# Strassen loop of a hybrid decoder layer: the operand sums T1 and T3 are made by accumulating transfers instead of VectorE subtractions

## What is computed

```python
D_FF = -(-(8 * D_MODEL) // (3 * 256)) * 256          # 5632
h2 = rms_norm(x, norm2_gain[layer]) * (1 + sc2) + sh2
ffn = (jax.nn.silu(h2 @ ffn_w_gate[layer]) * (h2 @ ffn_w_up[layer])) @ ffn_w_down[layer]
x = x + g2 * ffn
```

## Time and profile before

| | |
|---|---|
| median of 3 executions | 2366.89 us |
| profiled execution | 2369.26 us |
| its span, first to last instruction | 2367.6 us |
| mean granted TensorE clock | 0.993 |
| TensorE matmul busy | 2317.0 us (98%) |
| VectorE busy | 1640.9 us (69%) |
| ScalarE busy | 832.5 us (35%) |
| GpSimd busy | 82.5 us (3%) |
| DMA engines, mean busy share | 49.8% for the queue of SyncE |

### The profile page before, as it was taken

How to read it: one execution, slowest core, us unless ns; L and a number is a source line. 1 busy time by engine, 2 the same in 40 slices (tenths; PEclk the granted TensorE clock), 3 DMA queues, 4 the chain that set the end, 5 groups by cost and what they waited for, 6 DMA issues and landing times.

```text
span 2367.6 us, 28777 instructions
## 1 busy us (share of the span) xinstructions
PE 2317.0 (98%) x10544; PEld 1868.4 (79%) x10544; DVE 1640.9 (69%) x2057; ACT 832.5 (35%) x1147; POOL 82.5 (3%) x80
## 2 busy tenths in 40 slices
PE   6999999999999999999999999999999999999998
PEld 5877787788876788788878787878787878887877
DVE  5976876587757433666777777776868686868683
ACT  4233324343236322343333333333424242424232
POOL 0012100021001000000000000000000000000000
PEclk8999999999999999999999999999999999999999
DMA  9976681677640143234444445353445353545452
GB/s 341 321 263 222 238 306 61 230 237 262 205 145 19 53 161 98 86 110 143 162 134 156 159 151 166 126 179 129 161 133 186 124 180 122 166 142 170 138 164 81
DMA packets 233745, 392.36 MB, mean 166 GB/s; under 512 B 16441, under 2 KB 108063, under 8 KB 232520
## 3 DMA queue, kind: packets, MB, share of 16 engines
q1 hardware_dynamic: 233672, 391.39, 49.8%
HBM read 382.93 MB, written 11.03 MB: 166 GB/s over the span
## 4 chain that ended last, share of the span: by engine, by line
PE 85%; DVE 7%; issue 3%; ACT 2%; DMA 2%; SPq 1%; DVEq 0%; ACTq 0%
PE PS L1057 11%; PE PS L1059 10%; PE PS L1058 10%; PE PS L1112 7%; PE PS L1114 7%; PE PS L1113 7%; PE PS L676 6%; PE PS L678 6%; PE PS L677 6%; PE PS L840 2%; PE PS L683 2%; PE PS L684 2%; PE PS L685 2%; PE PS L816 2%; DVE acc_first L1611 1%
## 5 line engine op out<-in xcount | busy, mean ns | idle before, releaser
L1452 ACT ACTIVATE whi<-stage 128x1024 fp32r<-128x1024 f32 x368 | 390.7, 1062 | 840.6 <-PE PS L1059 444.8
L2000 DVE TENSOR_TENSOR wlo<-stage,whi 128x1024 fp32r<-128x1024 f32 x368 | 449.8, 1224 | 181.0 <-ACT whi L1452 181.0
L1057 PE MATMUL PS<-whi,xc_hi 128*128 128x512 f32 x1216 | 480.8, 395 | 3.2 <-DVE g_tok L2102 2.2
L1059 PE MATMUL PS<-whi,xc_lo 128*128 128x512 f32 x1216 | 474.7, 390 | 0.0
L1058 PE MATMUL PS<-wlo,xc_hi 128*128 128x512 f32 x1216 | 474.3, 390 | 0.0
L1560 DVE TENSOR_TENSOR wlo<-stage,whi 128x1024 fp32r<-128x1024 f32 x136 | 173.1, 1274 | 217.8 <-ACT whi L1230 217.7
L676 PE MATMUL PS<-hhi,whi 128*128 128x512 f32 x768 | 311.3, 405 | 7.5 <-DVE wlo L1560 4.6
L678 PE MATMUL PS<-hhi,wlo 128*128 128x512 f32 x768 | 303.0, 395 | 0.0
L677 PE MATMUL PS<-hlo,whi 128*128 128x512 f32 x768 | 302.8, 394 | 0.0
L1230 ACT ACTIVATE whi<-stage 128x1024 fp32r<-128x1024 f32 x136 | 144.2, 1062 | 437.9 <-PE PS L678 308.6
L1057 PEld LDWEIGHTS PS<-whi,xc_hi 128*128 128x128 f32 x1216 | 228.1, 188 | 77.4 <-DVE wlo L2000 7.5
(11 more groups left out here) (297 smaller groups left out, 2481.7 us busy)
## 6 DMA issues: line engine op xcount, KB each, us to landing
stage<-in_ffn_w_up SPq DMA_DIRECT2D x168, 512.0 KB, 4.0
ada_ring<-in_ada_w SPq DMA_DIRECT2D x128, 512.0 KB, 4.9
stage<-in_ffn_w_gate SPq DMA_DIRECT2D x128, 512.0 KB, 3.7
stage<-in_ffn_w_down SPq DMA_DIRECT2D x88, 512.0 KB, 4.6
stage<-in_w_in SPq DMA_DIRECT2D x80, 512.0 KB, 6.1
ada_first<-in_ada_w SPq DMA_DIRECT2D x64, 512.0 KB, 6.7
stage<-in_w_out SPq DMA_DIRECT2D x32, 512.0 KB, 3.7
xnat<-in_x SPq DMA_DIRECT2D x4, 1024.0 KB, 8.0
```

Source lines behind the costliest of these rows:

```text
L1057: mm(PS[:, b, :], x_hi, w, start=start, stop=False)
L1059: return mm(PS[:, b, :], x_lo, w, start=False, stop=stop)
L1452: f(whi[:, p % NW, :, :].rearrange("p k n -> p (k n)"), slot_of(p), ACT.Copy).then_inc(w_hi, 1)
L2000: v.tensor_tensor(wlo[:, p % NW, :, :].rearrange("p k n -> p (k n)"), slot_of(p), whi[:, p % NW, :, :].rearrange("p k n -> p (k n)").bitca ...
```

## The change

The signs of the scheme are turned so that T1 and T3 are plain sums: T1 = b12 + b11 and T3 = b12 + b22, of the weights as they lie in memory. Then T2 = b22 + T1, and the third and fourth become b11 + T3 and b21 more. The left-hand S1, S2 and S4 change sign to match, and so do U, the first block's product with SiLU (now a `SCALAR_TENSOR_TENSOR` with -1) and the output gate `mod[:, 5, :]`, which is negated once.

T1 and T3 are not made by VectorE any more. SyncE loads the first piece into the slot as before. GpSimd waits for its landing and issues a second transfer of 512 KB from the weights in HBM with `accum_op=ALU.add` into the same slot: `add_weights`, eight for each block, 80 in all, written out one after another without a loop. It also waits for the landing of the accumulating transfer two before it, since two counters (`added`) take turns. ScalarE's copy of a T1 or T3 position, and VectorE's sums that read it, wait for that counter. `sel_ready` and `silu_done` are folded into other counters to make room. The load into position 15 waits for the `wlo` of position 9 and no more for a sum.

```diff
-FREED_BY = {1: 4, 3: 7, 6: 8, 9: 14, 14: 19, 24: 27, 28: 31, 32: 35}
+FREED_BY = {1: 4, 3: 7, 6: 8, 14: 19, 24: 27, 28: 31, 32: 35}
+ADDED = (1, 3, 6, 14, 21, 25, 29, 33)
...
+        def added_at(n, p):
+            return 16 * (ADDED.index(p) // 2 + 1 + 4 * n)
...
                 if p in SUMMED and not down:
                     act.wait_ge(w_sum, sums_of(n, p))
+                elif p in ADDED and not down:
+                    act.wait_ge(added[ADDED.index(p) % 2], added_at(n, p))
                 else:
...
-            then(v.tensor_tensor(t16[:, 0:GCH], mod[:, 3, 0:GCH], mod[:, 3, GCH:KT], ALU.add))
+            then(v.tensor_tensor(t16[:, 0:GCH], mod[:, 3, GCH:KT], mod[:, 3, 0:GCH], ALU.subtract))
+            then(v.tensor_scalar(mod[:, 5, :], mod[:, 5, :], -1.0, None, ALU.mult))
             dve.wait_ge(rh_done, 1)
...
-            def t1(n, j):
-                b11, p, _ = SET1[j]
-                in_stage(n, b11, p)
-                v.tensor_tensor(slot_of(p), slot_of(p), slot_of(b11), ALU.subtract).then_inc(w_sum, 1)
...
-            def t3(n, j):
-                _, p, b22, _ = SET2[j]
-                in_stage(n, p, b22)
-                v.tensor_tensor(slot_of(p), slot_of(b22), slot_of(p), ALU.subtract).then_inc(w_sum, 1)
...
             def b11_plus_t3(n, j):
                 _, t3_at, _, p = SET2[j]
-                in_stage(n, p)
-                dve.wait_ge(w_sum, sums_of(n, t3_at))
+                in_stage(n, t3_at, p)
                 v.tensor_tensor(slot_of(p), slot_of(p), slot_of(t3_at), ALU.add).then_inc(w_sum, 1)
...
-                    v.tensor_tensor(g_tok[:, t, :], PS[:, 4 + t, :], silu_0[:, t, :], ALU.mult
-                                    ).then_inc(bank_free[4 + t], 1)
+                    v.scalar_tensor_tensor(out=g_tok[:, t, :], in0=PS[:, 4 + t, :], scalar=-1.0, in1=silu_0[:, t, :],
+                                           op0=ALU.mult, op1=ALU.mult).then_inc(bank_free[4 + t], 1)
...
+            def add_weights(n, p, w, half, j):
+                i = ADDED.index(p)
+                if n or i >= 2:
+                    pool.wait_ge(added[i % 2], added_at(n, p) - 16)
+                pool.wait_ge(stage_in[p % NRING], landed_at(n, p))
+                g.dma_start(slot_of(p).rearrange("p (k n) -> p k n", k=CK),
+                            w[:, half, CK * j:CK * j + CK, CW * n + CW:CW * n + 2 * CW],
+                            accum_op=ALU.add).then_inc(added[i % 2], 16)
+
+            for n in range(NFB - 1):
+                for j in range(4):
+                    add_weights(n, SET1[j][1], gate_w, 0, j)
+                for j in range(4):
+                    add_weights(n, SET2[j][1], up_w, 1, j)
```

More of the change, by code:

```diff
@@ L283, in hybrid_layer @@
         lags_ready, table_pe, table_sb = sem("lags_ready"), sem("table_pe"), sem("table_sb")
-        silu_done = sem("silu_done")
+        added = [sem(f"added{b}") for b in range(2)]
         mod2_pe, mod2_done = sem("mod2_pe"), sem("mod2_done")
@@ L389, in sums_of @@
         def sums_of(n, p):
-            first = sorted(p for js in SET1 for p in js[1:])
+            first = [js[2] for js in SET1]
             if p in first:
[L393 to L398, removed]
+                return first.index(p) + 1 + 12 * n
+            return 4 + 2 * [js[3] for js in SET2].index(p) + 2 + 12 * n
+        SUMMED = [js[2] for js in SET1] + [js[3] for js in SET2]
         def f_of(f):
@@ L1957, in x_sums @@
                 dve.wait_ge(h2_t, 2 * kp + 2)
-                v.scalar_tensor_tensor(out=b[:, S1, :], in0=b[:, A21, :], scalar=t16[:, kp:kp + 1], in1=b[:, A22, :],
-                                       op0=ALU.add, op1=ALU.add).then_inc(x_sum, 1)
+                v.scalar_tensor_tensor(out=b[:, S1, :], in0=b[:, A22, :], scalar=t16[:, kp:kp + 1], in1=b[:, A21, :],
+                                       op0=ALU.add, op1=ALU.subtract).then_inc(x_sum, 1)
                 v.tensor_tensor(b[:, S3, :], b[:, A11, :], b[:, A21, :], ALU.subtract).then_inc(x_sum, 1)
@@ L1962, in x_sums @@
                 v.scalar_tensor_tensor(out=b[:, S2, :], in0=b[:, S1, :], scalar=low, in1=b[:, A11, :],
+                                       op0=ALU.add, op1=ALU.add).then_inc(x_sum, 1)
+                dve.wait_ge(x_sum, n + 3)
+                v.scalar_tensor_tensor(out=b[:, S4, :], in0=b[:, S2, :], scalar=high, in1=b[:, A12, :],
                                        op0=ALU.subtract, op1=ALU.subtract).then_inc(x_sum, 1)
-                dve.wait_ge(x_sum, n + 3)
-                v.scalar_tensor_tensor(out=b[:, S4, :], in0=b[:, A12, :], scalar=high, in1=b[:, S2, :],
-                                       op0=ALU.add, op1=ALU.subtract).then_inc(x_sum, 1)
             def x_low(kp):
@@ L2005, in in_stage, with t4 @@
                 for p in ps:
-                    dve.wait_ge(stage_in[p % NRING], landed_at(n, p))
-            def t1(n, j):
-                b11, p, _ = SET1[j]
-                in_stage(n, b11, p)
-                v.tensor_tensor(slot_of(p), slot_of(p), slot_of(b11), ALU.subtract).then_inc(w_sum, 1)
-            def t2(n, j):
-                _, first, p = SET1[j]
-                in_stage(n, p)
-                dve.wait_ge(w_sum, sums_of(n, first))
-                v.tensor_tensor(slot_of(p), slot_of(p), slot_of(first), ALU.subtract).then_inc(w_sum, 1)
-            def t3(n, j):
-                _, p, b22, _ = SET2[j]
-                in_stage(n, p, b22)
-                v.tensor_tensor(slot_of(p), slot_of(b22), slot_of(p), ALU.subtract).then_inc(w_sum, 1)
+                    if p in ADDED:
+                        dve.wait_ge(added[ADDED.index(p) % 2], added_at(n, p))
+                    else:
+                        dve.wait_ge(stage_in[p % NRING], landed_at(n, p))
+            def t2(n, j):
+                _, t1_at, p = SET1[j]
+                in_stage(n, t1_at, p)
+                v.tensor_tensor(slot_of(p), slot_of(p), slot_of(t1_at), ALU.add).then_inc(w_sum, 1)
             def b11_plus_t3(n, j):
                 _, t3_at, _, p = SET2[j]
-                in_stage(n, p)
-                dve.wait_ge(w_sum, sums_of(n, t3_at))
+                in_stage(n, t3_at, p)
                 v.tensor_tensor(slot_of(p), slot_of(p), slot_of(t3_at), ALU.add).then_inc(w_sum, 1)
-            def minus_t4(n, j):
-                b21, t3_at, _, p = SET2[j]
+            def t4(n, j):
+                b21, _, _, p = SET2[j]
                 in_stage(n, b21)
-                dve.wait_ge(w_sum, sums_of(n, t3_at) + 1)
-                v.tensor_tensor(slot_of(p), slot_of(b21), slot_of(p), ALU.subtract).then_inc(w_sum, 1)
+                dve.wait_ge(w_sum, sums_of(n, p) - 1)
+                v.tensor_tensor(slot_of(p), slot_of(p), slot_of(b21), ALU.add).then_inc(w_sum, 1)
             p_base, r_base = uses(16) + 1, uses(15) + 1
@@ L2292, in _ @@
                     then(last)
-            last.then_inc(sel_ready, 1)
+            last.then_inc(consts, 1)
             def sum_squares(n, dst):
```

26 lines of the change are left out of this document (9 added, 17 removed).

## The result

The changed kernel took 2383.39 us, the median of four executions (2381.51 to 2386.05), beside 2367.91 us for the kernel before (four executions, 2366.37 to 2369.16). The ratio is 1.0068 with a 95% interval of 1.0053 to 1.0083: 15.5 us, or 0.7%, slower. The forecast was 2365.5 us and no change to be seen, 2362 to 2371. The wide range, 2361 to 2415, holds the result; the forecast itself does not. The profiled execution took 2383.32 us over a span of 2381.6 us, at a mean granted clock of 0.993 as before, so the clock is no part of it.

The account below looks back on a forecast made before the run. TensorE was taken to bound the kernel. Profiled execution: 2369.3 - 1.0 - 0.5 + 0.1 = 2367.9 us; median: 2366.9 - 1.4 = 2365.5 us, no visible change (2362 to 2371), wide range 2361 to 2415.

Parts of the forecast that it names:

- What bounds the kernel: Whole run: TensorE, busy 2317.0 of 2367.6 us; VectorE mostly arrives in time, so relieving it pays only where it is late.
- The gain of 1.5 us: Sums removed from VectorE: TensorE's step at position 2 gains 1.0 us over nine blocks, the loop's start 0.5 us.
- VectorE's busy time: 80 sums of 1.22 us leave VectorE: busy time falls by some 98 us to about 1543.
- The price of an accumulating transfer: GpSimd's added transfers: 4.5 + 1.3 us plus up to 1 us for issue, 6 to 7 us each.
- a load on the engines: DMA engines: each added transfer takes 2.6 us of every engine; share rises to 0.74 in SET2, about 0.85 in SET1.
- the budget: Tightest slot, position 3: 8.3 us left after the first landing against 6 to 7 us needed, 1.3 to 2.3 us over.
- 7 us or more later: GpSimd's queue: only the next transfer waits behind a waiting one, and its first piece is loaded 7 us or more later.
- Rival A: Second transfer late at position 3, over 8.3 us landing to landing; TensorE stops: +13 us, 2379, at 9.6 us; chance 0.33.
- Rival B: Ordinary loads late before VectorE's sums, 1 us in four places a block: 40 us, 2406; chance 0.10.
- Rival C: VectorE's lighter load lets all TensorE gaps close: 22 us faster, 2345; chance 0.05.
- The shared interface: VectorE's two-input SBUF sums might hold up GpSimd's descriptor writing, turning 6.5 us into 10.2; would strengthen Rival A.

Follow-up runs that it names:

- position 3 alone: Changed kernel with one accumulating transfer a block, at position 3, the other seven sums back on VectorE: 2374.89 us, ratio 1.0034 to the kernel before.
- all but 1: Changed kernel with only position 1's sum back on VectorE, seven accumulating transfers a block: 2381.83 us, ratio 1.0059 to the kernel before.
- position 1 alone: Changed kernel with one accumulating transfer a block, at position 1, the other seven sums back on VectorE: 2368.79 us, ratio 1.0004 to the kernel before.
- with the loads exchanged: Changed kernel with SyncE issuing position 3's load ahead of position 2's in every block but the first: 2391.47 us, ratio 1.0101 to the kernel before.
- position 33 alone: Changed kernel with one accumulating transfer a block, at position 33, the other seven sums back on VectorE: 2367.85 us, ratio 1.0002 to the kernel before.
- the run of six transfers: Changed kernel with accumulating transfers only at positions 1, 6, 14, 21, 25 and 29, sums of 3 and 33 on VectorE: 2367.38 us, ratio 0.9998.

## Why the prediction was wrong, by its own steps

**What bounds the kernel**: right. TensorE's busy time did not move, and 65 us less work on VectorE bought nothing.

**The gain of 1.5 us**: its parts are seen where no late transfer hides them. In the run with position 3 alone TensorE goes into position 2 in steps of 0.22 and 0.23 us, without the 0.34 of before, and in the changed kernel the 0.77 us step at the start of the loop is gone; the step there is 0.23. They are too small for a median to show.

**VectorE's busy time**: forecast 1543, measured 1552.4. The sums ran back to back with their neighbours, whose records overlap: 1560.22 to 1561.35 is 1.13 us from start to start, not 1.22. 80 x 1.13 = 90.4 is what their removal could take off the busy time, and that is nearly the 88.5.

**The price of an accumulating transfer**: right when alone, and this misled. Landing to landing it takes 0.54 us until GpSimd starts plus 5.9, 6.4 us in all, inside the forecast 6 to 7, at positions 14, 21, 25 and 29 (medians). As a load on the engines it was set too low at 2.6 us of each: by the page it is 2381.6 x 0.106 / 80 = 3.2 us of every engine for one transfer, and 2364.0 x 0.057 / 80 = 1.7 for a copy from GpSimd.

**The step that failed** is the budget: "The load of position 3 is issued at 1550.03 and lands 4.5 us later ... 8.3 us are left", against 6 to 7 us, "It fits, with 1.3 to 2.3 us over". Both sides of it were read with the engines nearly free, the first landing from the trace before and the second from rows of that trace, and the added load was then spread over whole stages, 0.85 for SET1. That average was about right (0.81 was measured), and it says nothing of the 14.5 us around the two copies, where the share is 1.03. In the changed kernel it is the first term that broke at position 3: the load lands in 7.6 us, 3.1 later than the 4.5 of the budget, and eats the 1.3 to 2.3 us over; the added transfer itself takes 6.5 us from landing to landing, as forecast. In company the terms are these:

| medians, us | first landing | GpSimd starts | second landing | needed | issue to copy, before | gap to the next load |
|---|---|---|---|---|---|---|
| position 3, changed kernel | 7.6 | 0.54 | 5.95 | 14.1 | 12.8 | 5.1 |
| position 3, all but 1 | 4.5 | 0.54 | 8.4 | 13.4 | 12.8 | 1.4 |
| position 3 alone | 4.5 | 0.54 | 8.6 | 13.7 | 12.8 | 1.5 |
| position 1, changed kernel | 6.2 | 0.54 | 8.1 | 14.85 | 14.05 | 0.5 |
| position 1 alone | 4.8 | 0.54 | 5.9 | 11.2 | 14.05 | 1.4 |
| position 29, changed kernel | 3.5 | 0.54 | 5.8 | 9.8 | 14.05 | 2.6 |

("Issue to copy" is from the load's issue to ScalarE's copy in the kernel before, the median of the same nine blocks; "GpSimd starts" is from landing to issue; the gap is from GpSimd's issue to SyncE's next. Ordinary loads are under way when GpSimd starts at position 3, and none is at positions 1 and 29.) Whichever way, position 3 needs 0.6 to 1.3 us more than it has. When its first piece is on time, the second has ordinary loads under way before it and the load of position 6 close behind it, and takes 2.5 to 2.7 us longer; when position 1's transfer is in the way, the first piece is 3.1 us late and no load comes close behind the second. At position 3 the delay could be moved and not removed, as the runs without position 1 and with the loads exchanged show; at position 1 leaving out position 33 removes it.

Two smaller slips are in the same step. Position 6 has no budget at all; it had room in the change but was late in five blocks of "all but 1". And the next first piece on GpSimd's queue is not "7 us or more later" everywhere: the load of position 6 is issued 6.5 us behind that of 3 in the trace of before, and in the change the two accumulating transfers start 4.0 us apart and are in flight together for 1.9 us.

**Rival A** (a late second transfer at position 3, chance 0.33, 2379 us) had the right consequence: ScalarE holds the copy, VectorE the `wlo`, and TensorE stops. Its condition, over 8.3 us from landing to landing, holds with position 3 alone (9.2) and in "all but 1" (8.9), but not in the changed kernel, where it is 6.5. Its price for 9.6 us was 1.3 us a block; at positions 1 and 3 the table of stops has 2.9 + 8.7 = 11.6 us, 1.3 us in each of nine blocks, because the 3 us that were missing came in before, with the first piece. That this sum agrees so well is luck. **Rival B** (late ordinary loads before VectorE's sums, 0.10) came true beside it in part, in the 2.8 us at position 33. That late loads bite was right, and its size, 40 us, and its condition were not: it bites at one place and in five blocks of nine, with engines held for 3.2 us and not 5, and 0.4 us a block on VectorE costs next to nothing, as position 33 alone shows. That an ordinary load would be late as the first piece of a sum, which is what position 3 pays for, stands in neither. They were weighed as separate cases and are one: the same full stretch makes both the added and the ordinary transfers late. **Rival C** did not come true: the run of six transfers has the lighter VectorE and no loss, and gains nothing that can be measured.

**The shared interface** of VectorE and GpSimd, which the Trainium skill describes in "SBUF — State Buffer", section "Who interferes with whom", played no part that can be seen: GpSimd's instruction took 1203 ns as minimum and as median in the 36 gate transfers shown, beside VectorE's sums all along. The Trainium skill infers there that writing descriptors is not hit by sums with two SBUF inputs, and this trace agrees. The opposite would have given the 10.2 us from landing to landing that the prediction named; the longest in the changed kernel was 9.0.

What stays open: in which order the engines took the packets of the two queues, and so why the same transfer varies by 1.8 us from block to block at position 3, where the gap to the next load varies only from 1.2 to 1.6 us. The landings were measured, the order was not.

## What to carry to other kernels

Before adding a transfer to a loop, write down for the tightest slot who else is in flight between its issue and its use, and price both it and them in that company: a transfer that needs 5.9 us alone took 7 to 9 with ordinary loads under way before it or with the next one issued less than 1.1 us behind it, and made a load just behind it up to 3 us later. Look at the gap to the next issue of the other queue, and follow the delay around the loop: position 33 alone cost nothing, and made position 1 late. A DMA share averaged over a stage hides this; take it over the few microseconds in which the tight use falls. And offloading an engine that is not waited for pays nothing even when it is free, so the only open question about such a change is what it costs.

## What was not expected of the hardware

- An accumulating transfer of 512 KB into SBUF holds the DMA engines for 3.2 us each, a copy of the same bytes from the same queue for 1.7 us, and the copy lands in 4.2 us where the addition lands in 5.9. The Trainium skill, in "Collectives: The Full Stack", section "The bandwidth ceiling: the fold count and why AG ≠ RS ≠ AR", says of the addition in a reduce-scatter between cores that it is slower because it needs two source reads, at about half the rate of the copying collective. Here the ratio agrees, 10.6% against 5.7% of the engines' time; no run shows that the second read is the reason.
- An accumulating transfer that starts with no load under way landed in 5.6 to 6.3 us when SyncE's next load came 1.2 us or more behind it, and in 6.9 to 8.5 when it came less than 1.1 us behind (positions 1, 29 and 33).
- GpSimd's own instruction is longer with the addition, 1203 ns against 724 ns, which may be 0.5 of the 1.7 us between their landings; it wasn't tried apart.
- GpSimd starts 0.54 us after the landing that it waits for, by the median at every position; in single blocks of the changed kernel it was 0.30 to 1.28.
